# Third layer of a two-block model: the delta rule's levels, tail and preparation interleaved over chunks, key norms moved among the projection's slabs, convolution sums in PSUM

## The reference, cut to what matters

```
def even_mixer(h, w_in, conv_a_w, dn_conv_w, ...):
    p = h @ w_in                                    # 1024 -> 3592 columns
    a_gate_in, a_gate_out, a_h, qkv, z, beta_raw, alpha_raw = split(p)
    y_a = a_gate_out * causal_dwconv(a_gate_in * a_h, conv_a_w)      # 3 taps
    qkv = silu(causal_dwconv(qkv, dn_conv_w))                        # 4 taps
    q, k = l2_norm(q) * 128**-0.5, l2_norm(k)       # 4 heads of 128
    beta, g = sigmoid(beta_raw), -exp(a_log) * softplus(alpha_raw + dt_bias)
    o = gated_delta_rule(q, k, v, beta, g)
    y_b = rms_norm(o, dn_norm_w) * silu(z)
    return concatenate([y_a, y_b]) @ w_out

def gated_delta_rule(q, k, v, beta, g):  # chunkwise: a triangular solve in
    # each chunk, then S = exp(g_last) S + k_dec^T v_new from chunk to chunk
```

## Time and profile before

| | |
|---|---|
| time, median of 3 runs | 2939.32 us (2938.93 to 2939.33) |
| profiled execution | 2945.55 us, span 2943.8 us |
| PE busy | 2752.9 us, 94% |
| mean granted clock of PE | 0.932 of full speed |
| slabs of `even` | to 1497.9 us of the span |
| beta/alpha product | to 1517.4 us |
| l2 norms | to 1547.36 us |
| recurrence | 1547.36 to 1793.04 us |
| head norm, until PE's next slab | to 1815.8 us |

### The profile page before, as it was taken

One profiled execution on the slowest core, in us unless ns is written; L12 is line 12 of the kernel. 1 busy time (PEld: TensorE's weight loads), 2 busy tenths in 40 slices (PEclk: granted clock), 3 DMA queues, 4 the chain that ended last, 5 costly groups with the idle time before them and its releaser, 6 DMA issues.

```text
span 2943.8 us, 51052 instructions
## 1 busy us (share of the span) xinstructions
PE 2752.9 (94%) x18058; PEld 2432.1 (83%) x18058; DVE 1050.5 (36%) x1928; ACT 936.8 (32%) x2090; POOL 1201.4 (41%) x1007
## 2 busy tenths in 40 slices
PE   7979999999999999999986666999999999999998
PEld 7857888888967888889975556999999866999998
DVE  3263211221163221254644443441442255342340
ACT  4274322232274322342231112322233355322221
POOL 4444444444463444444431112444444342444443
PEclk9999999999998999999976778999999955999999
DMA  4212222322131232222210000222222100222222
GB/s 159 68 44 65 93 98 88 98 95 92 43 65 43 93 100 88 97 102 86 86 43 1 0 0 14 93 88 90 86 98 80 62 5 1 79 93 93 86 91 88
DMA packets 80372, 212.99 MB, mean 72 GB/s; under 512 B 30224, under 2 KB 32912, under 8 KB 80272
## 3 DMA queue, kind: packets, MB, share of 16 engines
q1 hardware_dynamic: 80272, 211.69, 22.8%
HBM read 209.57 MB, written 2.10 MB: 72 GB/s over the span
## 4 chain that ended last, share of the span: by engine, by line
PE 69%; issue 15%; POOL 8%; DVE 6%; ACT 2%; DVEq 1%; POOLq 0%; DMA 0%; SPq 0%; ACTq 0%
PE ps L1040 51%; POOL w_lo L508 7%; PE ps L1055 4%; PE ps L1264 4%; PE ps L1183 2%; PE ps L1166 2%; PE ps L1153 2%; DVE s_sb L1387 1%; PE ps L1249 1%; PE ps L1187 1%; PE ps L1234 1%; POOL bias_sb L586 1%; DVE p_t L1372 1%; ACT z_m L988 1%; DVE x_m L1362 0%
## 5 line engine op out<-in xcount | busy, mean ns | idle before, releaser
L508 POOL TENSOR_TENSOR w_lo<-raw,w_hi 128x512 fp32r<-128x512 f32 (+1 forms) x704 | 981.8, 1416 | 1206.5 <-ACT w_hi L701 1206.4
L1040 PE MATMUL ps<-h_hi,w_hi 128*128 128x264 f32 (+1 forms) x3296 | 872.0, 321 | 15.1 <-POOL h_lo L654 8.0
L701 ACT ACTIVATE w_hi<-raw 128x512 fp32r<-128x512 f32 (+1 forms) x704 | 426.5, 653 | 1430.5 <-PE ps L1040 1315.1
L1040 PE MATMUL ps<-h_lo,w_hi 128*128 128x264 f32 (+1 forms) x3296 | 871.4, 320 | 0.0
L1040 PE MATMUL ps<-h_hi,w_lo 128*128 128x264 f32 (+1 forms) x3296 | 869.0, 320 | 0.0
L1040 PEld LDWEIGHTS ps<-h_hi,w_hi 128*128 128x128 f32 x3296 | 549.7, 189 | 65.1 <-issue 16.9
L1040 PEld LDWEIGHTS ps<-h_lo,w_hi 128*128 128x128 f32 x3296 | 547.3, 189 | 45.6 <-issue 1.0
L1040 PEld LDWEIGHTS ps<-h_hi,w_lo 128*128 128x128 f32 x3296 | 547.7, 189 | 44.0
L1040 PE MATMUL ps<-act_lo,w_hi 128*128 128x264 f32 (+1 forms) x1056 | 282.4, 322 | 0.0
L1040 PE MATMUL ps<-act_hi,w_lo 128*128 128x264 f32 (+1 forms) x1056 | 282.0, 321 | 0.0
L1040 PE MATMUL ps<-act_hi,w_hi 128*128 128x264 f32 (+1 forms) x1056 | 280.9, 320 | 0.0
(11 more groups left out here) (233 smaller groups left out, 2989.6 us busy)
## 6 DMA issues: line engine op xcount, KB each, us to landing
raw<-slabs_d SPq DMA_DIRECT2D x288, 512.0 KB, 3.5
raw<-slabs_d SPq DMA_DIRECT2D x64, 704.0 KB, 4.0
rpb_raw<-rpb_d SPq DMA_DIRECT2D x24, 224.0 KB, 5.1
bias_sb<-alibi_d SPq DMA_DIRECT2D x6, 384.0 KB, 3.4
x<-x_d SPq DMA_DIRECT2D x1, 2048.0 KB, 12.9
out_d<-x SPq DMA_DIRECT2D x1, 2048.0 KB, 7.2
mem_in<-mem_d SPq DMA_DIRECT2D x1, 1024.0 KB, 7.2
dn_cst<-dn_consts_d SPq DMA_DIRECT2D x1, 640.0 KB, 5.0
```

What stands on the lines that cost most here:

```text
L508: nc.gpsimd.tensor_tensor(w_lo[:, s, a * P:b * P], raw[:, s, a * P:b * P], w_hi[:, s, a * P:b * P].bitcast(f32), ALU.subtract).then_inc(lo ...
L701: nc.scalar.activation(w_hi[:, s, a * P:b * P], raw[:, s, a * P:b * P], ACT.Copy)\
L1040: last = nc.tensor.matmul(ps[:, s * 2 * BANK + po:s * 2 * BANK + po + n], w[:, s, wk], a[:, k, to:to + n], start=(k == 0 and w is w_hi and ...
```

## The change

Four things are rewritten, all in the third layer.

1. The slab order of `even` becomes q, k, v (12), z (4), the beta/alpha product, then the gated convolution's pairs (8) and its output gate (4).
2. The stage `tn l2` is gone. Its eight tiles' norms stand inside `even`: one after each of the 8 pair slabs.
3. `taps` writes its running sum to PSUM, `acc(2)` or `acc(3)`, not to SBUF; ACT's SiLU reads it there.
4. `delta` is written out as rounds. In the six pieces of a round r stand level i of chunk r, piece i of chunk r-1's tail, and piece i of chunk r+1's preparation. Buffers that more than one chunk needs are doubled or tripled; `kc` and `vc` are no longer copied. `gated_split` and the split of the next two slabs move on POOL to behind the masks of chunk 0.

```
-    add("tn", what="l2", n=8)
-    add("delta")
+    add("delta", pre=norms[-1])
...
+        def rounds():
+            for r in range(-1, len(CHUNKS) + 1):
+                for i in range(PIECES):
+                    here = Chunk(r) if 0 <= r < len(CHUNKS) and i < len(levels_of(r)) else None
+                    old = Chunk(r - 1) if r >= 1 else None
+                    new = Chunk(r + 1) if r + 1 < len(CHUNKS) else None
+                    yield here, old, new, i
...  # POOL
+                    if k.c == 0:
+                        gated_split(st)
+                        stream(st.slab0 + 2)
...  # ACT, even
+                silu(0)
+                with act.Fori(1, 6) as i:
+                    for s in range(RING):
+                        split_hi(i + (q0 + 1), s)
+                    silu(i)
...
+                for j in range(8):
+                    s = j % 2
+                    nc.scalar.activation(sq[:, s, :], qkv[:, j, :], ACT.Square).then_inc(tn_sq, 1)
+                    split_hi(q0 + 9 + j // 2, s)
+                    act.wait_ge(tn_ms, st.tn0 + j + 1)
+                    if j >= 2:
+                        act.wait_ge(tn_out, st.tn0 + j - 1)
+                    nc.scalar.activation(halves_of(root[:, s, :], 2), acc(3, 2), ACT.Ln, bias=eps_col)\
+                        .then_inc(tn_rt, 1)
...  # PE, even
-                many(st.slab0 // 2 + 1, 13, 2, hi, lo)
+                many(q0 + 1, 7, 2, hi, lo)
...
+                pe.wait_ge(ba_dve, 4)
+                for j in range(8):
+                    slab(q0 + 8 + j // 2, j % 2, 2, hi, lo)
+                    pe.wait_ge(tn_sq, st.tn0 + j + 1)
+                    for po, to, m in chunks(2):
+                        last = nc.tensor.matmul(ps[:, 6 * BANK + po:6 * BANK + po + m], ones, sq[:, j % 2, to:to + m],
+                                                start=True, stop=True)
+                    last.then_inc(tn_ms, 1)
+                many(q0 + 12, 2, 2, hi, lo)
...  # PE, delta
+                for here, old, new, i in rounds():
+                    if here:
+                        first_product(here, here.levels[i])
+                    if old:
+                        tail(old, i)
+                    if here:
+                        second_products(here, here.levels[i])
+                    if new:
+                        pre(new, i)
...  # DVE, even
+                        taps(acc(2 + s, 2), padded[:, s, :], [dn_taps[:, 2 * i + s, k:k + 1] for k in range(4)], ev_in,
+                             6 * i + 3 * s).then_inc(ev_conv, 1)
...  # DVE, delta
+                def pre(k, i):
+                    n, done = k.n, d_sem["pre", "dve"]
+                    if i == 0:
+                        after(k, "pre", "pe", "rows")
...
+                    if i == 5:
+                        tt(k.x_m[k.sq4], a_m[k.sq4], all_heads(first_level, n), ALU.mult).then_inc(done, 1)
+                        tt(k.x_m[k.sq4], all_heads(ident, n), k.x_m[k.sq4], ALU.subtract).then_inc(done, 1)
+                        tt(k.x_t[k.sq4], k.a_t[k.sq4], all_heads(first_level_t, n), ALU.mult).then_inc(done, 1)
+                        tt(k.x_t[k.sq4], all_heads(ident, n), k.x_t[k.sq4], ALU.subtract).then_inc(done, 1)
```

More of the change, by code:

```diff
@@ L283, in build @@
         four = [P, DN_H, P]
[L284 to L288, removed]
+        gb, row, dt_, dl_, a_m, z_m, k_dec, q_dec, state = (
+            small(n, four, f32, 0 if n == "gb" else None)
+            for n in ("gb", "row", "dt_", "dl_", "a_m", "z_m", "k_dec", "q_dec", "state"))
+        a_ts, x_ms, x_ts = ([small(f"{n}{e}", four) for e in range(2)] for n in ("a_t", "x_m", "x_t"))
+        qk_ts, erows = ([small(f"{n}{e}", four) for e in range(3)] for n in ("qk_t", "erow"))
         a_lv = small("a_lv", [P, 2, DN_H, P])
-        dn_cst = small("dn_cst", [P, d["dn_consts"].shape[1]])
+        dn_cst = small("dn_cst", [P, d["dn_consts"].shape[1]], f32, 12200)
+        res, v_new = big("res", four, f32, wide_at[0] + 20 * TOK), big("v_new", four)
+        r1 = q_dec
         after_eq, before = (dn_cst[:, i * P:(i + 1) * P] for i in range(2))
@@ L297, in build @@
         gate, beta = sb("gate", [P, 5, DN_H]), sb("beta", [P, 5, DN_H])
-        dcol, edec, dlast, elast, bed, ea = (sb(n, [P, DN_H]) for n in ("dcol", "edec", "dlast", "elast", "bed", "ea"))
+        dcol, dlast, bed, ea = (sb(n, [P, DN_H]) for n in ("dcol", "dlast", "bed", "ea"))
+        edecs, elasts = sb("edec", [P, 3, DN_H]), sb("elast", [P, 3, DN_H])
         w_ba = sb("w_ba", [P, DT, 8])
@@ L355, in build @@
             sem(n) for n in ("head_step", "head_ready", "head_hi", "head_lo", "gated_hi", "gated_lo"))
-        d_pe, d_dve, d_act, d_pool = sem("d_pe"), sem("d_dve"), sem("d_act"), sem("d_pool")
+        d_sem = {(part, engine): sem(f"{part}_{engine}") for part in ("pre", "levels", "tail")
+                 for engine in ("pe", "dve", "act", "pool")[:4 if part == "levels" else 3]}
         stored = sem("stored")
@@ L371, in peeled, with __init__, after @@
                     body(i)
[L373 to L383, removed]
+        class Chunk:
+            def __init__(self, c):
+                self.c, (self.t0, self.n) = c, CHUNKS[c]
+                self.tok = slice(self.t0, self.t0 + self.n)
+                self.levels = levels_of(c)
+                self.a_t, self.x_m, self.x_t = a_ts[c % 2], x_ms[c % 2], x_ts[c % 2]
+                self.qk_t, self.erow = qk_ts[c % 3], erows[c % 3]
+                self.edec, self.elast = edecs[:, c % 3, :], elasts[:, c % 3, :]
+                self.sq4 = (slice(0, self.n), slice(None), slice(0, self.n))
+            def after(self, engine, part, maker, name):
+                engine.wait_ge(d_sem[part, maker], dn_at[part, maker, self.c, name])
+        def rounds():
[5 more added lines that the diff above has]
+                    yield here, old, new, i
         class Pair:
@@ L1844, in delta @@
                 wait(loaded, 16 * N_LOADS + 16)
                 fill(state[:, :, :], 0.0)
-                chunk(0, META)
-                with loop(1, 5) as c:
-                    chunk(c, P)
+                spread_gate(Chunk(0))
+                for here, old, new, i in rounds():
+                    if here:
+                        level(here, here.levels[i])
+                    if old:
+                        tail(old, i)
+                    if new:
+                        pre(new, i)
```

494 lines of the change are left out of this document (249 added, 245 removed).

## The result

| | before | after |
|---|---|---|
| time, median | 2939.12 us (4 runs, 2936.47 to 2939.33) | 2861.91 us (4 runs, 2859.37 to 2863.0) |
| profiled execution | 2945.55, span 2943.8 | 2859.37, span 2857.6 |
| mean granted clock | 0.932 | 0.947 |

The ratio is 0.9734 (95% interval 0.972 to 0.9748): 77.2 us less, where 2863 with a range of 2846 to 2888 had been forecast. From here on the profiled execution is used for places, the medians for sums. The kernel before was measured again beside each later group of kernels, and its median there was 2942.82, 2941.37, 2941.73 and 2938.77 us. So a difference between two kernels of different groups is sure to some 4 us only, and the kernel after belongs to the first group alone.

What follows compares the result with a forecast made beforehand. Dense products on PE were taken to bound most of the kernel, its chain the recurrence. Recurrence 59.5, norms 15.9 and convolution sums 0.5 sum to 75.9 us less: 2863 from a median of 2939.32, range 2846 to 2888.

Steps and rivals of the forecast that it cites:

- The recurrence, 59.5 less: Delta recurrence: tail and preparation go into the gaps of the levels, 186 us against 245.7.
- The walk of the queues: Recurrence: each round's cost worked out by following the four engine queues in their new order with durations of before.
- The round, 40.0: Full round of the recurrence, z to z: 40.0 us against 54.7 a chunk, with half clock for 6 us.
- signs of being wrong: Recurrence: the forecast is wrong if the rounds take over 45 us or under 36.
- The row of ten: Round's end: ten DVE instructions in a row, not PE, are late next; last pitch 10.3 us.
- First part, 27, and last part, 39.3: Recurrence's ends: chunk 0's preparation and short levels beside chunk 1's preparation 27 us; last two chunks' remainder 39.3.
- Norms, 15.9: l2 norms: 29.96 us go and 14.1 come in their place, 15.9 us less, from 11 to 20.
- Convolution sums, 0.5: Convolution slabs, sums in PSUM: net 0.5 us less, between 1 more and 1.5 less.
- 1, the lock in full: Rounds: each GpSimd mask costs DVE the full 1.1 us, up to 4.2 a round more, 2880 us; chance 0.13.
- 2, full clock over the pause: Rounds: the clock stays up over PE's 7 us pause, 17 us less, 2846 us; chance 0.07.
- 3 and 4, half clock in the rounds or from the beta/alpha product on: PE at half clock: throughout the rounds, 2937 us, chance 0.05; from beta/alpha to the recurrence's end, 3007, chance 0.03.
- 5: Rounds: some wait ties a round to the tail before it, so parts don't overlap; no size or chance of its own.

Runs made afterwards that it cites:

- short_masks: The kernel after, but GpSimd's level masks cover one head of four, so only the time is of use: 2850.96 us.
- v1: The kernel after with the copies of output and a_t on ACT, and a round's first product waiting for x_m, not x_t: 2834.7 us, ratio to before 0.964.
- v3: v1 with two more copies on ACT (row, gb) and x_m's first two instructions ahead of the state update on DVE: 2826.39 us, ratio to before 0.9607.
- conv_sbuf: The kernel after with the convolution sums back in SBUF, all else kept: 2862.6 us.
- filler6: The kernel after with six groups of four unused products on PE between the last and first product of three rounds: 2851.28 us.
- norms_stage: The kernel after with the eight norms and the beta/alpha product behind the slabs again, as a stage of their own: 2876.12 us.
- late_split: The kernel after with gated_split and the slab stream behind it moved on GpSimd from behind chunk 0's masks to behind the last chunk's: 2857.39 us.

## Why the prediction was right, and where it was not

- **The recurrence, 59.5 less.** In the profile 245.7 became 185.1, 60.5 less. By the runs it is 43.1 of overlap and 17.6 of the two copies and the early `gb`, 60.7 (39 and 21 by the ratios to before). The forecast of the whole was right; its first sentence, which gave all of it to filling the levels' gaps, was not. The walk of the queues had both in it, but nowhere did I price the copies by themselves.
- **The round, 40.0.** It was 37.7. The pitches from z to z were 7.6, 5.0, 5.8, 5.6, 4.1 and 9.6, against 9.1, 5.2, 5.8, 5.5, 4.1 and 10.3. One term was mis-sized: half clock lasted 4.2 us, not 6, 1.5 less. The last pitch was 0.7 shorter, since the lock took 1.2 us there and not 2; in the whole round it cost 2.1, near the 2.3 that was estimated from the earlier trace rows (short_masks). The other four pitches are right to 0.2 us, in part by luck: they hold 0.9 us of lock, where the sum had 0.3. The round stayed within the two bounds named as signs of being wrong, 36 and 45.
- **What is late next.** The row of ten, as said, though the z behind it reads only `x_m`; the last two instructions of the row were a wait that could be moved, and v1 moved it: v1 and v3 took instructions out of it and the round fell to 31.4 and 29.7.
- **First part, 27, and last part, 39.3.** 28.0 and 40.3 (from z to the recurrence's end). `gated_split` cost 3.8, not 2. Chunk 1's round was 41.2, not 40. The full rounds were 2.3 and 2.0 better than forecast, these three 1.0, 1.0 and 1.2 worse. That the errors nearly cancel is luck.
- **Norms, 15.9.** 14.2 by the medians, 15.2 by the profile, the move of the beta/alpha product included. PE waited 1.03 us for DVE, not 1.5; half clock lasted 4.6 us, not 5.3.
- **Convolution sums, 0.5.** Mis-sized: 0.7 to 3.8. The loss that I read in the earlier trace rows came from DVE being behind in two windows at the end of the convolutions (11.60 and 10.78 of 11.74 us); in the new order the convolutions come first and each pair of slabs would lose 0.1 to 0.9 (conv_sbuf). That POOL's splits lengthen a convolution instruction into SBUF is in before's trace: the TENSOR_SCALAR from 1421.06, beside a split, takes 1.59 us. Into PSUM, in after's, the one from 1347.50 takes 0.77 beside a split, and all sixteen average 0.772. The bound of 1.5 was too narrow if the profiled 3.8 is the right figure.
- **Rivals.** 1, the lock in full: refuted by short_masks (2.1, not 6.6 a round). 2, full clock over the pause: refuted; the 4.2 us behind the three pauses of 6.2 to 6.7 us are at 0.50, 0.50 and 0.56, and filler6 shows what that costs (2.0 us of the round). 3 and 4, half clock in the rounds or from the beta/alpha product on: PEclk is 1.00 in the pair slabs and 0.91 in a round. 5: nothing ties the parts.

By the medians the four parts add up: 43.1 + 17.6 + 14.2 + 0.7 = 75.6 of 77.2. That it comes so close is partly luck, since each of them can be off by some 4 us; by the ratios to before they sum to 69.

## What to carry to other kernels

When two pieces of work fill the gaps of a third, don't add what each would hide: here 9.1 and 9.8 us a chunk made 13.0. Once they overlapped, the period was set by the engine with the longest row ahead of the shared point (here DVE's ten instructions: 37.7 us a round, and 31.4 with four of them out of the way); count that row and move its instructions to an idle engine, since half clock behind the wait cost time too (2.0 us a round here). Check too whether the shared point needs the whole row: here the last two instructions were waited for and not read. Price a removed copy by what is queued behind it, not by its own length: three of 0.43 us were 4 us a chunk here. And when a run is to price one cost, look whether another moved with it: a longer stretch at half clock hid a third of what the lock cost.

## What the hardware showed that I had not expected

**A short instruction lasted until the long one beside it was over.** In the beta/alpha part of before a VectorE instruction on 128 x 20 took as long as it took GpSimd to finish; the same one in norms_stage, with GpSimd idle, took 0.18. Before, then norms_stage:

```profile
1518.26 1.21 DVE L1357 SCALAR_TENSOR_TENSOR dn_s<-dn_s 128x20 f32<-128x20 f32 x1
```

```profile
1509.12 0.18 DVE L1427 SCALAR_TENSOR_TENSOR dn_s<-dn_s 128x20 f32<-128x20 f32 x1
```

GpSimd's subtraction of `gated_split` ran from 1518.14 to 1519.44; the instruction ended at 1519.47. Before's next one of this shape does the same: from 1520.11 it takes 1.31 us, to 1521.42, beside a subtraction from 1520.08 to 1521.39, and in norms_stage 0.18 (1509.94). In both the price was that of the rest of GpSimd's instruction, not of VectorE's own size.

**A copy with one input took longer too.** `gb<-gate` takes 0.43 us alone (after, 1628.24), and in v1 1.32 us beside a mask (1617.19, the mask from 1616.89 to 1618.23). It goes the other way too: at 1584.18 in v1 both start together, and there the copy takes 0.43 us and the mask 1.54, where the one from 1598.57 in before, with VectorE idle, takes 1.26.

**The clock dips without a pause ahead of it.** In chunk 1's round of after, between two products that waited about a microsecond at most, two stretches ran at half clock: a group from 1564.35 took 2.08 us, and one from 1575.35 1.92, both at 0.50. The same instructions took 1.16 and 1.06 in conv_sbuf and filler6. From the `rows` product in chunk 1's round to that in chunk 2's it was 40.9 us in after, 41.1 in late_split and 41.2 in norms_stage, but 37.7 in conv_sbuf. Shortly ahead of both stand products of chunk 0's tail, which are 16 rows or columns wide (from 1563.28 and 1570.41), and the rounds of chunks 2 and 3, whose tails are full, have none. But conv_sbuf and filler6 issue the same narrow products and keep full clock. Nothing in the edits explains it, and it alone moves a single execution by 3 us, more than the convolution sums are worth. Why it comes in some executions stays open.
